# The long filter of a Hyena layer: hidden layers made inside the projection, sum and difference folded into the output weights, one sum over partitions

## The chip, the cores and the metric

The kernel runs on one core of one Trainium2 chip. The metric is the time of the whole kernel on the device, in microseconds. Three runs of the kernel before took 2927.18, 2945.96 and 2937.9 us, a median of 2937.9.

## The reference

The program is a two-layer encoder on 1024 positions of 1024 channels in float32: normalisation, a mixer, a residual, and a mixture of experts, twice. The mixer of the first layer is half attention and half a Hyena operator. The operator convolves a sequence `z` with a filter as long as the sequence, through Fourier transforms. The change concerns how this filter is computed:

```python
z = concat([t, cos(ang), -sin(ang)])          # (1024, 33), constants
hdn = sin(freq * (z @ w1 + b1))               # (1024, 64)
hdn = sin(freq * (hdn @ w2 + b2))             # (1024, 64)
filt = hdn @ w3                               # (1024, 2 * 512): forward and backward
decay = exp(-t * deltas)                      # (1024, 512)
h_fwd, h_bwd = filt[:, :512] * decay, filt[:, 512:] * decay
kern = concat([h_fwd.at[0].add(h_bwd[0]), zeros, h_bwd[:0:-1]])
kern = kern / (sum(abs(kern), axis=0) + EPS)
y = irfft(rfft(z_seq) * rfft(kern)) + z_seq * skip
```

For real transforms of both directions the kernel needs `hs = h_fwd + h_bwd` and `hd = h_fwd - h_bwd`, and for the division the sum of |h_fwd| + |h_bwd| over positions, in which position 0 counts as |h_fwd + h_bwd|.

## The kernel before

The kernel is a row of phases. Each phase is a function that writes one instruction list for each engine, with waits on semaphores by hand; it ends with `end_phase()`, a barrier of all engines. So work of two phases never overlaps, except that the big weights arrive through a ring of three chunks of 2 MB, refilled by SyncE as products finish (`refill`, L166).

Four phases matter here. `hyena_project` (L919) makes 12 blocks of the projection, three groups of four. A step is 48 matmuls of 512 columns into two of the PSUM banks 0 to 5; beside it ScalarE copies the block before into `up` and splits the next weights, VectorE runs the three-tap convolution (L1078 to L1091), and in the first eight steps the attention's output is normalised and transposed through banks 6 and 7 (`turn`, `move`). TensorE's list is: product i, then `turn(i)`.

`hyena_filter` (L1098) loads eight small tables on SyncE's queue (L1124), and all engines wait for all of them. TensorE then makes layer one, transposes half of `z` (`turn`), makes layer two, transposes the rest; VectorE brings each layer's argument into the range of the sine in six operations on 64 partitions of 1024 columns (L1242 to L1251), ScalarE takes the sine (L1212). Then come eight steps of 128 positions each: two filter matmuls with 64 rows (L1172), forward and backward; VectorE multiplies each by the decay (L1259, L1260) and forms sum and difference (L1261, L1262); ScalarE takes the sizes of both directions (L1198); TensorE sums them over partitions with a column of ones (L1162, `norm_sum`), two matmuls a step into one row. At the end this row becomes a column of reciprocals (L1264 to L1266), and ScalarE multiplies `z` by `skip` (L1226).

A float32 matmul shows as two records in the trace, each with its own weight load; those on `fp32r` data as one, and a transpose as one.

`hyena_forward` (L1276) loads transform tables piece by piece on SyncE's queue and makes 33 results, each evacuated by ScalarE (`keep`, L1338), from which VectorE forms four groups of products. `hyena_inverse` reads `z` for the skip term.

Of the kernel before, what the change touches and what calls it, by code (L numbers as in the profile page):

```python
# [8 lines left out]
F32R = mybir.dt.float32r  # L9
# [60 lines left out]
def build(nc, I, out):  # L70
    ctx = ExitStack()
    with ctx:
# [846 lines left out]
        def hyena_project(z, yT, xnH, o, gain, post):  # L919

            (proj, padded, convolved, weights_in, edges, chain, x_high, x_rest, w_high, w_rest,
             gain_in, squared, mean_ok, root_ok, scaled, turned, copied) = take(17)
            with ExitStack() as st:
# [7 lines left out]
                wH = sb(st, "w_high_hy", [P, 2, KD, P], F32R)  # L931
                STEPS = 3 * HC
                TURN = 6

# [13 lines left out]
                with nc.Block() as block:  # L948
                    @block.sync
                    def _(sp):  # L950
                        sp.dma_start(g_bc[:], gain.partition_broadcast(P)).then_inc(gain_in, 16)
                        sp.dma_start(cw[:], I["hy_conv_w"]).then_inc(weights_in, 16)
                        sp.dma_start(cb[:], I["hy_conv_b"]).then_inc(weights_in, 16)
                        refill(sp, S_HY, S_OUT0, proj, HC)

                    @block.tensor
                    def _(pe):
                        def turn(j):
# [6 lines left out]
                            last.then_inc(turned, 1)  # L965

                        for i in range(STEPS):
# [12 lines left out]
                            if i < NT:  # L980
                                turn(i)

                    @block.scalar
                    def _(act):
                        def squares(j):
# [32 lines left out]
                        for i in range(STEPS):  # L1018
# [11 lines left out]
                            if i < NT:  # L1030
                                move(i)

                    @block.vector
                    def _(dve):
                        did = Tally(chain)

# [33 lines left out]
                        for i in range(STEPS):  # L1070
# [27 lines left out]
        def hyena_filter(z, zT, hs, hd, hinv):  # L1098
            (tab_in, lin, argued, waved, filt, decayed, mixed, normed, turned, moved, skipped, chain,
             row_ok, summed, patched) = take(15)  # L1100
            with ExitStack() as st:
                zp = sb(st, "hy_positions", [EMB, T])
                w1 = sb(st, "hy_w1", [EMB, FF])
                w2 = sb(st, "hy_w2", [FF, FF])
                w3 = sb(st, "hy_w3", [FF, 2 * 512])
                fb = sb(st, "hy_fb", [FF, 3])
                tneg = sb(st, "hy_tneg", [P, NT])
                delta = sb(st, "hy_delta", [P, 512])
                skip = sb(st, "hy_skip", [P, HC])
                arg = sb(st, "hy_arg", [FF, T])  # L1110
                turns = sb(st, "hy_turns", [FF, T])
                hdn = sb(st, "hy_hidden", [FF, T])
                dec = sb(st, "hy_decay", [P, 2, 512])
                hf = sb(st, "hy_fwd", [P, 2, 512])
                hb = sb(st, "hy_bwd", [P, 2, 512])
                ab = sb(st, "hy_abs", [P, 2, 2, 512])
                row = sb(st, "hy_row", [1, 512])
                TWO_PI = 2 * np.pi
                HI = 6.28125
                LO = TWO_PI - HI  # L1120
                MAGIC = 1.5 * 2.0 ** 23
                with nc.Block() as block:
                    @block.sync
                    def _(sp):  # L1124
                        for t, src in ((zp[:], I["c_positions"]), (w1[:], I["hy_w1"]), (w2[:], I["hy_w2"]),
                                       (w3[:], I["hy_w3"]), (fb[:], I["hy_fb"]), (tneg[:], I["c_tneg"]),
                                       (delta[:], I["c_delta"].partition_broadcast(P)), (skip[:], I["hy_skip"])):
                            sp.dma_start(t, src).then_inc(tab_in, 16)

                    @block.tensor  # L1130
                    def _(pe):
                        def layer(w, x):
                            for half in range(2):
                                last = nc.tensor.matmul(psum[0:FF, half, :], w[:], x[:, half * 512:(half + 1) * 512],
                                                        start=True, stop=True)
                            last.then_inc(lin, 1)

                        def turn(n):
                            par, mt = divmod(n, NF)
                            if n >= 4:  # L1140
                                pe.wait_ge(moved, n - 3)
                            for ct in range(HC):
                                t0 = par + 2 * mt * P
                                last = nc.tensor.transpose(psum[:, 4 + n % 4, ct * P:(ct + 1) * P],
                                                           z[:, ct, t0:t0 + 2 * P - 1:2], ident[:])
                            last.then_inc(turned, 1)

                        pe.wait_ge(tab_in, 16 * 8)
                        layer(w1, zp)
                        for n in range(4):  # L1150
                            turn(n)
                        pe.wait_ge(waved, 1)
                        layer(w2, hdn)
                        for n in range(4, NT):
                            turn(n)
                        pe.wait_ge(waved, 2)
                        pe.wait_ge(moved, NT)

                        def norm_sum(n):
                            pe.wait_ge(mixed, n + 2)  # L1160
                            for d in range(2):
                                last = nc.tensor.matmul(psum[0:1, 4, :], ones[:, 0:1], ab[:, n % 2, d, :],  # L1162
                                                        start=(n == 0 and d == 0), stop=(n == NT - 1 and d == 1))
                            last.then_inc(normed, 1)

                        for n in range(NT):
                            par, mt = divmod(n, NF)
                            t0 = par + 2 * mt * P
                            if n >= 2:
                                pe.wait_ge(summed, n - 1)  # L1170
                            for half in range(2):
                                last = nc.tensor.matmul(psum[:, 2 * (n % 2) + half, :], hdn[:, t0:t0 + 2 * P - 1:2],  # L1172
                                                        w3[:, half * 512:(half + 1) * 512], start=True, stop=True)
                            last.then_inc(filt, 1)
                            if n:
                                norm_sum(n - 1)
                        norm_sum(NT - 1)
                        pe.wait_ge(row_ok, 1)
                        for ct in range(HC):
                            last = nc.tensor.matmul(psum[:, 5, ct:ct + 1], row[0:1, ct * P:(ct + 1) * P],  # L1180
                                                    ones[0:1, 0:1], start=True, stop=True)
                        last.then_inc(normed, 1)

                    @block.gpsimd
                    def _(pool_e):
                        pool_e.wait_ge(patched, 2)
                        nc.gpsimd.memset(ab[0:1, 0, 1, :], 0.0).then_inc(mixed, 1)

                    @block.scalar
                    def _(act):  # L1190
                        def size(n):

                            b = n % 2
                            act.wait_ge(summed, n + 1)
                            if n >= 2:
                                act.wait_ge(normed, n - 1)
                            for d, h in ((0, hf), (1, hb)):
# [1703 lines left out]
```

## Time and profile before

| | |
|---|---|
| median of three runs | 2937.9 us |
| the profiled execution | 2935.33 us, span 2933.5 us |
| TensorE matmul busy | 2554.4 us (87%) |
| VectorE busy | 1860.2 us (63%) |
| ScalarE busy | 1448.1 us (49%) |
| GpSimd busy | 441.0 us (15%) |
| mean granted TensorE clock | 0.927 |

Engines are named PE (TensorE), DVE (VectorE), ACT (ScalarE), POOL (GpSimd) and SP (SyncE); SPq is SyncE's queue of loads. Busy is the time in which instructions ran. A granted clock of 1.0 is 2.4 GHz, 0.5 is 1.2 GHz. In a timeline a row gives start and duration in us, engine, line, operation, output and inputs, the shape, how many instructions were merged (x), and in brackets how long the engine was idle before and what ended that. In a row of stretches the columns are: stretch, length, busy us and count of PE, PEld (weight loads), DVE, ACT and POOL, then granted clock, share of the DMA engines and GB/s.

### The profile page before, as it was taken

The numbers are of one execution on the slowest core, as the hardware profiler recorded it, in microseconds if no ns is written. First come the engines' busy times: TensorE is split into PE (matmuls) and PEld (weight loads), VectorE is DVE, ScalarE is ACT, GpSimd is POOL, SyncE is SP. The second block draws the span as 40 slices with busy tenths as digits, with TensorE's granted clock in tenths as the row PEclk, the third lists the DMA queues.
The fourth block names the chain that finished last, engine by engine and source line by source line (L and its number), as shares of the span: only waits on it lengthen the run. The fifth ranks groups of instructions, "written<-read, shape, count | busy, mean of one in ns | idle before, by whom it ended". The sixth has DMA issues, their size and how long they took to land. (4 is left out here: it accounts for less than half of the span.)

```text
span 2933.5 us, 34401 instructions
## 1 busy us (share of the span) xinstructions
PE 2554.4 (87%) x12440; PEld 2021.0 (69%) x12440; DVE 1860.2 (63%) x2221; ACT 1448.1 (49%) x1731; POOL 441.0 (15%) x396
## 2 busy tenths in 40 slices
PE   5989898797893999999985999879494899999994
PEld 4768786243571788888874899867382688888882
DVE  5748754455334888888874310079734789888980
ACT  4338731311220778878864222143511678877870
POOL 0001000000000133333310000012200233332320
PEclk9989998798996999999997999979697899999997
DMA  4110001011131899999992101200322699999992
GB/s 159 46 43 2 5 29 67 7 36 72 65 143 38 334 382 389 384 377 387 385 331 77 58 30 51 94 1 1 129 94 83 253 378 377 379 375 378 401 341 96
DMA packets 86674, 533.41 MB, mean 182 GB/s; under 512 B 18503, under 2 KB 24135, under 8 KB 61096
## 3 DMA queue, kind: packets, MB, share of 16 engines
q1 hardware_dynamic: 63240, 494.17, 42.8%
q0 software_dynamic: 18720, 33.61, 4.8%
q10 hardware_dynamic: 4608, 4.20, 0.4%
q8 instruction: 68, 1.11, 0.2%
q14 instruction: 38, 0.31, 0.0%
HBM read 511.45 MB, written 55.05 MB: 193 GB/s over the span
## 5 line engine op out<-in xcount | busy, mean ns | idle before, releaser
L1936 DVE TENSOR_TENSOR wL<-ring,wH 128x2048 fp32r<-128x2048 f32 x384 | 869.0, 2287 | 140.2 <-ACT wH L1883 134.8
L1883 ACT CAST wH<-ring 128x2048 fp32r<-128x2048 f32 x384 | 730.2, 1910 | 227.8 <-DMA ring<-in_moe_w 161.1
L1802 PE MATMUL psum<-wH,xgH 128*128 128x512 f32 x1024 | 408.4, 399 | 8.9 <-DVE xgL L1936 8.7
L1804 PE MATMUL psum<-wH,xgL 128*128 128x512 f32 x1024 | 401.4, 392 | 0.0
L1810 PE MATMUL psum<-wL,xgH 128*128 128x512 f32 x1024 | 274.7, 390 | 0.0
L1802 PEld LDWEIGHTS psum<-wH,xgH 128*128 128x128 f32 x1024 | 193.4, 189 | 52.3 <-DVE xgL L1936 7.8
L1810 PEld LDWEIGHTS psum<-wL,xgH 128*128 128x128 f32 x1024 | 192.5, 188 | 41.4
L1804 PEld LDWEIGHTS psum<-wH,xgL 128*128 128x128 f32 x1024 | 193.6, 189 | 38.5
L1802 PE MATMUL psum<-wH,hidH 128*128 128x512 f32 x512 | 207.7, 406 | 10.4 <-DVE hidL L1936 10.4
L1804 PE MATMUL psum<-wH,hidL 128*128 128x512 f32 x512 | 201.6, 394 | 0.0
L190 PE MATMUL psum<-w_high_vo,xn_high 128*128 128x256 f32 x512 | 144.1, 281 | 5.4 <-DVE ring_rest L185 5.4
L192 PE MATMUL psum<-w_high_vo,xnT_rest 128*128 128x256 f32 x512 | 144.3, 282 | 0.0
L191 PE MATMUL psum<-ring_rest,xn_high 128*128 128x256 f32 x512 | 144.2, 282 | 0.0
L1810 PE MATMUL psum<-wL,hidH 128*128 128x512 f32 x512 | 137.4, 390 | 0.0
L192 PE MATMUL psum<-xn_high,ring_rest 128*128 128x512 f32 x320 | 127.3, 398 | 0.0
L1757 POOL COPY gidx<-slots 128x1 int32 (+1 forms) x64 | 55.1, 860 | 479.7 <-PE psum L1819 479.5
L1802 PEld LDWEIGHTS psum<-wH,hidH 128*128 128x128 f32 x512 | 97.3, 190 | 29.8 <-DVE hidL L1936 10.9
L190 PE MATMUL psum<-w_high,xnT_rest 128*128 128x512 f32 x256 | 103.0, 402 | 14.4 <-DVE ring_rest L185 14.4
L1810 PEld LDWEIGHTS psum<-wL,hidH 128*128 128x128 f32 x512 | 96.8, 189 | 20.4
L1804 PEld LDWEIGHTS psum<-wH,hidL 128*128 128x128 f32 x512 | 97.6, 191 | 18.4
L191 PE MATMUL psum<-ring_rest,xnT_rest 128*128 128x512 f32 x256 | 101.7, 397 | 0.0
L192 PE MATMUL psum<-w_high,yT_rest 128*128 128x512 f32 x256 | 101.5, 397 | 0.0
(407 smaller groups left out, 4965.0 us busy)
## 6 DMA issues: line engine op xcount, KB each, us to landing
ring<-in_moe_w SPq DMA_DIRECT2D x192, 2048.0 KB
ring<-in_ev_w_in SPq DMA_DIRECT2D x6, 2048.0 KB
ring<-in_od_w_in SPq DMA_DIRECT2D x6, 2048.0 KB
xn_scratch<-xn_out SPq DMA_DIRECT2D x16, 512.0 KB, 3.6
ow<-in_moe_w SPq DMA_DIRECT2D x3, 2048.0 KB, 12.4
x_all<-in_x SPq DMA_DIRECT2D x4, 1024.0 KB, 8.1
ring<-in_ev_w_out SPq DMA_DIRECT2D x2, 2048.0 KB
dft_tables<-in_c_dft SPq DMA_DIRECT2D x16, 256.0 KB, 3.0
```

Of the source, the lines that this page charges most:

```text
L190: nc.tensor.matmul(dst, lhs[0], rhs[0], start=start, stop=False)
L191: nc.tensor.matmul(dst, lhs[0], rhs[1], start=False, stop=False)
L192: return nc.tensor.matmul(dst, lhs[1], rhs[0], start=False, stop=stop)
L1757: nc.gpsimd.tensor_copy(idx[:, b:b + 1], slots[:, bass.ds(e, 1)]).then_inc(idx_ok, 1)
L1802: nc.tensor.matmul(psum[:, bank, :], xh[:, k, :], w3[0][:, n, cols], start=(half == 0 and n == 0), stop=False)
L1804: nc.tensor.matmul(psum[:, bank, :], xl[:, k, :], w3[0][:, n, cols], start=False, stop=False)
L1810: ins = nc.tensor.matmul(psum[:, bank, :], xh[:, k, :], w3[1][:, n, cols], start=False, stop=(half == 1 and n == len(ks) - 1))
L1883: nc.scalar.copy(half_of(wH, b, e, c, half), raw(e, c, half)).then_inc(w_high, 1)
L1936: return nc.vector.tensor_tensor(out, whole, high.bitcast(F32), ALU.subtract)
```

## The change

It does five things. The two sine layers move into `hyena_project`: after the products of steps 7 to 10 TensorE makes one half (512 positions) of a layer each, with the weights doubled to 128 columns, so that the hidden values stand twice, on partitions 0 to 63 and 64 to 127; banks 6 and 7 and the buffer `sq` are reused. The tables are loaded there. The output weights are combined once: rows 0 to 63 of `w3` become forward plus backward, rows 64 to 127 forward minus backward. So in `hyena_filter` one matmul on the lower rows gives the sum and one on the upper rows the difference, and one product with the decay each gives `hs` and `hd`. The sizes are computed from |h_fwd| + |h_bwd| = max(|hs|, |hd|) (`both_abs`, `larger`), added up over the eight steps by GpSimd, and summed over partitions once. The transposes of `z` alternate with the filter matmuls, evacuated by ScalarE and VectorE in turn. The scaling by `skip` moves to pieces 3 to 6 of `hyena_forward`, with its load.

The diff, cut:

```diff
@@ hyena_project
+                        for t, src in ((zp, I["c_positions"]), (w1, I["hy_w1"]), (w2, I["hy_w2"]), (fb, I["hy_fb"]),
+                                       (w3, I["hy_w3"][0]), (tneg, I["c_tneg"]),
+                                       (delta, I["c_delta"].partition_broadcast(P))):
+                            sp.dma_start(t[:], src).then_inc(mlp_in, 16)
                         refill(sp, S_HY, S_OUT0, proj, HC)
...
+                        def hidden_layer(u):
+                            if u == 0:
+                                pe.wait_ge(mlp_in, 16 * 7)
+                            if u < 2:
+                                pe.wait_ge(copied, NT - 1 + u)
+                            else:
+                                pe.wait_ge(argued, u - 1)
+                                pe.wait_ge(waved, u - 1)
+                            w, x = (w1, zp) if u < 2 else (w2, hidden[0:FF, :])
+                            nc.tensor.matmul(psum[:, TURN + u % 2, :], w[:], x[:, piece(u)], start=True, stop=True
+                                             ).then_inc(lin, 1)
...
                             last.then_inc(proj, 1)
                             if i < NT:
                                 turn(i)
+                            if MLP <= i < MLP + 4:
+                                hidden_layer(i - MLP)
...
+                        def wave(u):
+                            act.wait_ge(argued, u + 1)
+                            nc.scalar.activation(hidden[:, piece(u)], sq[:, 0, :], ACT.Sin).then_inc(waved, 1)
...
+                            if i == MLP - 2:
+                                act.wait_ge(squared, NT)
+                                act.dma_start(w3b, I["hy_w3"][1]).then_inc(back_in, 16)
+                            if MLP <= i < MLP + 4:
+                                wave(i - MLP)
...
+                        def argument(u):
+                            V, k = nc.vector, u // 2
+                            arg, turns = sq[:, 0, :], sq[:, 1, :]
+                            dve.wait_ge(lin, u + 1)
+                            if u:
+                                dve.wait_ge(waved, u)
...
+                        def both_directions():
...
+                            for s, op in ((0, ALU.add), (1, ALU.subtract)):
+                                rows = slice(s * FF, (s + 1) * FF)
+                                nc.vector.tensor_tensor(w3[rows, :], w3[rows, :], w3b[rows, :], op).then_inc(summed, 1)
...
+                            if i == MLP - 1:
+                                both_directions()
+                                dve.wait_ge(squared, NT)
+                            if MLP <= i < MLP + 4:
+                                argument(i - MLP)
@@ hyena_filter, TensorE
+                        def filters(n):
...
+                            if n >= 2:
+                                pe.wait_ge(mixed, 2 * n - 2)
+                            for s in range(2):
+                                rows = slice(s * FF, (s + 1) * FF)
+                                last = nc.tensor.matmul(psum[:, 2 * (n % 2) + s, :], hidden[rows, t0:t0 + 2 * P - 1:2],
+                                                        w3[rows, :], start=True, stop=True)
                             last.then_inc(filt, 1)
...
+                        for n in range(NT):
+                            filters(n)
+                            turn(n)
+                        pe.wait_ge(gathered_up, NT - 1)
+                        nc.tensor.matmul(psum[0:1, SUM, :], ones[:, 0:1], total[:], start=True, stop=True
+                                         ).then_inc(normed, 1)
@@ hyena_filter, ScalarE
+                        decay(0)
+                        for n in range(NT):
+                            if n + 1 < NT:
+                                decay(n + 1)
+                            act.wait_ge(mixed, 2 * n + 2)
+                            if n >= 2:
+                                act.wait_ge(sized, n - 1)
+                            for s, h in ((0, hs), (1, hd)):
+                                nc.scalar.activation(both_abs[:, n % 2, s, :], h[:, n, :], ACT.Abs).then_inc(absolute, 1)
...
+                            if n % 2 == 0:
+                                act.wait_ge(turned, n + 1)
+                                nc.scalar.copy(zT[:, n, :], psum[:, 4, :]).then_inc(moved[0], 1)
@@ hyena_filter, GpSimd
+                        for n in range(1, NT):
+                            pool_e.wait_ge(sized, n + 1)
+                            if n > 1:
+                                pool_e.wait_ge(gathered_up, n - 1)
+                            nc.gpsimd.tensor_tensor(total[:], total[:], size[:, n % 2, :], ALU.add).then_inc(gathered_up, 1)
@@ hyena_filter, VectorE
+                        def larger(n):
+
+                            dve.wait_ge(absolute, 2 * n + 2)
+                            if n >= 3:
+                                dve.wait_ge(gathered_up, n - 2)
+                            nc.vector.tensor_tensor(size[:, n % 2, :] if n else total[:], both_abs[:, n % 2, 0, :],
+                                                    both_abs[:, n % 2, 1, :], ALU.max).then_inc(sized, 1)
+
                         for n in range(NT):
...
+                            nc.vector.tensor_tensor(hs[:, n, :], psum[:, 2 * b, :], dec[:, b, :], ALU.mult
+                                                    ).then_inc(mixed, 1)
+                            nc.vector.tensor_tensor(hd[:, n, :], psum[:, 2 * b + 1, :], dec[:, b, :], ALU.mult
+                                                    ).then_inc(mixed, 1)
+                            if n:
+                                larger(n - 1)
+                            if n % 2:
+                                dve.wait_ge(turned, n + 1)
+                                nc.vector.tensor_copy(zT[:, n, :], psum[:, 5, :]).then_inc(moved[1], 1)
@@ hyena_forward
+                        sp.dma_start(skip[:], I["hy_skip"]).then_inc(skip_in, 16)
                         for n in range(PIECES):
...
+                            if 3 <= n < 3 + HC:
+                                nc.scalar.activation(z[:, n - 3, :], z[:, n - 3, :], ACT.Copy, scale=skip[:, n - 3:n - 2]
+                                                     ).then_inc(skipped, 1)
```

## Rows read from the trace of the kernel before

**Rows 1.** Windows, projection and filter phase: stretch, length, busy us by engine.

```profile
367.50:493.80 126.30, 126.28 (x561) 101.94 (x558) 62.58 (x89) 32.92 (x84) 0.00 (x0) 1.00 0.09 34
499.10:576.60 77.50, 53.54 (x112) 18.33 (x112) 33.88 (x46) 27.48 (x41) 0.51 (x1) 0.70 0.05 16
```

**Rows 2.** Timeline of the filter phase: start us, us, engine, line, operation, [idle before].

```profile
497.03 1.28 DVE L1087 SCALAR_TENSOR_TENSOR yT<-u_padded,hy_conv_w,conv_acc 128x1024 f32<-128x1024 f32 x1
499.12 0.38 SPq L1128 DMA_DIRECT2D hy_positions<-in_c_positions  x1
...
505.85 3.67 PE L1134 MATMUL psum<-hy_positions,hy_w 33*64 33x512 f32 x4 [12.07 <-DMA hy_skip<-in_hy_skip]
...
521.72 3.69 PE L1144 MATMUL psum<-ident,z 128*128 128x128 f32 x16
...
530.97 7.16 PE L1172 MATMUL psum<-hy_w,hy_hidden 64*128 64x512 f32 x8 [5.56 <-ACT zT L1215]
```

**Rows 3.** Groups of instructions in the filter phase: busy, mean ns, idle before.

```profile
L1144 PE MATMUL psum<-ident,z 128*128 128x128 f32 x32 | 7.4, 422 | 0.0
...
L1219 ACT ACTIVATE hy_decay<-hy_delta,hy_tneg 128x512 f32<-128x512 f32 x8 | 5.6, 708 | 0.0
L1261 DVE TENSOR_TENSOR xnT<-hy_fwd,hy_bwd 128x512 f32<-128x512 f32 x8 | 5.5, 692 | 0.3
...
L1259 DVE TENSOR_TENSOR hy_fwd<-psum,hy_decay 128x512 f32<-128x512 f32 x8 | 5.5, 691 | 20.7 <-PE psum L1172 20.7
...
L1198 ACT ACTIVATE hy_abs<-hy_bwd 128x512 f32<-128x512 f32 x8 | 4.9, 612 | 0.0
...
L1219 ACT ACT_TABLE_LOAD x1 | 1.3, 1283 | 0.0
```

**Rows 4.** Timeline of the filter steps, TensorE.

```profile
550.07 1.99 PE L1172 MATMUL psum<-hy_w,hy_hidden 64*128 64x512 f32 x4
...
565.68 1.99 PE L1172 MATMUL psum<-hy_w,hy_hidden 64*128 64x512 f32 x4
```

**Rows 5.** Timeline, end of the filter phase.

```profile
571.54 4.25 ACT L1226 ACTIVATE z<-z,hy_skip 128x1024 f32<-128x1024 f32 x4
...
571.68 1.88 PE L1162 MATMUL psum<-hy_abs,ones 128*1 128x512 f32 x4 [2.21 <-ACT hy_abs L1198]
...
575.42 0.18 DVE L1266 RECIPROCAL hinv<-psum 128x4 f32<-128x4 f32 x1 [1.14 <-PE psum L1180]
```

**Rows 6.** Timeline, head norm of layer two, VectorE, then GpSimd.

```profile
2076.63 1.67 DVE L731 SCALAR_TENSOR_TENSOR xnT<-xnT,rs_ml,g_ml 128x256 f32<-128x256 f32 x4
...
2078.49 3.71 DVE L731 SCALAR_TENSOR_TENSOR xnT<-xnT,rs_ml,g_ml 128x256 f32<-128x256 f32 x4
...
2078.38 2.35 POOL L742 TENSOR_TENSOR xnT<-xnT,gate_ml 128x1024 f32<-128x1024 f32 x1 [28.84 <-DVE xnT L731]
```

**Rows 7.** Windows, TensorE alone: busy (records), PEclk the granted clock, DMA share.

```profile
498.00:500.00 2.00, 0.00 (x0) 0.53 1.07 459
524.50:525.50 1.00, 0.90 (x5) 0.54 0.00 0
531.00:538.20 7.20, 7.13 (x8) 0.50 0.00 0
550.00:571.00 21.00, 18.91 (x41) 1.00 0.00 0
```

**Rows 8.** Timeline of attention, TensorE.

```profile
254.36 0.40 PE L511 MATMUL psum<-k_high,q_rest 64*128 64x512 f32 x2
254.59 0.40 PE L511 MATMUL psum<-k_rest,q_high 64*128 64x512 f32 x2
```

**Rows 9.** Timeline of the forward transform, ScalarE and then VectorE.

```profile
641.27 0.66 ACT L1338 COPY filter_freq<-psum 128x512 f32<-128x512 f32 x1
...
696.11 2.50 DVE L1370 TENSOR_TENSOR freq_acc<-Z,filter_freq 128x512 f32<-128x512 f32 x4 [9.78 <-ACT filter_freq L1338]
```

More of the change, by code:

```diff
@@ L918, in hyena_project @@
         @phase
-        def hyena_project(z, yT, xnH, o, gain, post):
+        def hyena_project(z, yT, xnH, o, gain, post, hidden, consts):
             (proj, padded, convolved, weights_in, edges, chain, x_high, x_rest, w_high, w_rest,
-             gain_in, squared, mean_ok, root_ok, scaled, turned, copied) = take(17)
+             gain_in, squared, mean_ok, root_ok, scaled, turned, copied, mlp_in, lin, argued, waved, summed, back_in) = take(23)
+            w3, delta, tneg = consts
             with ExitStack() as st:
@@ L1093, in _, with hyena_filter @@
                                 scale(i + 1)
+                            if i == MLP - 1:
[3 more added lines that the diff above has]
+                                argument(i - MLP)
                 end_phase()
         @phase
-        def hyena_filter(z, zT, hs, hd, hinv):
-            (tab_in, lin, argued, waved, filt, decayed, mixed, normed, turned, moved, skipped, chain,
-             row_ok, summed, patched) = take(15)
-            with ExitStack() as st:
[L1102 to L1112, printed above, removed]
+        def hyena_filter(z, zT, hidden, consts, hs, hd, hinv):
+            (filt, decayed, mixed, absolute, sized, patched, gathered_up, normed, turned, moved0, moved1,
+             row_ok) = take(12)
+            moved = (moved0, moved1)
+            w3, delta, tneg = consts
+            with ExitStack() as st:
@@ L1120, in hyena_filter @@
-                LO = TWO_PI - HI
-                MAGIC = 1.5 * 2.0 ** 23
+                SUM = 6
                 with nc.Block() as block:
[L1123 to L1128, printed above, removed]
@@ L1130, in _ @@
                     @block.tensor
                     def _(pe):
[L1132 to L1164, printed above, removed]
@@ L1169, in _ @@
                             if n >= 2:
[L1170 to L1173, printed above, removed]
-                            last.then_inc(filt, 1)
-                            if n:
-                                norm_sum(n - 1)
@@ L1177, in _, with turn @@
-                        norm_sum(NT - 1)
+                                pe.wait_ge(mixed, 2 * n - 2)
[3 more added lines that the diff above has]
+                                                        w3[rows, :], start=True, stop=True)
+                            last.then_inc(filt, 1)
+                        def turn(n):
+                            par, mt = divmod(n, NF)
+                            if n >= 2:
+                                pe.wait_ge(moved[n % 2], n // 2)
+                            for ct in range(HC):
+                                t0 = par + 2 * mt * P
+                                last = nc.tensor.transpose(psum[:, 4 + n % 2, ct * P:(ct + 1) * P],
+                                                           z[:, ct, t0:t0 + 2 * P - 1:2], ident[:])
+                            last.then_inc(turned, 1)
@@ L1178, in _ @@
+                        for n in range(NT):
[4 more added lines that the diff above has]
+                                         ).then_inc(normed, 1)
                         pe.wait_ge(row_ok, 1)
                         for ct in range(HC):
-                            last = nc.tensor.matmul(psum[:, 5, ct:ct + 1], row[0:1, ct * P:(ct + 1) * P],
+                            last = nc.tensor.matmul(psum[:, SUM + 1, ct:ct + 1], row[0:1, ct * P:(ct + 1) * P],
@@ L1275, in hyena_forward @@
         @phase
-        def hyena_forward(zT, hs, hd, Z):
-            (done, copied, mixed, chain, early) = take(5)
+        def hyena_forward(z, zT, hs, hd, Z):
+            (done, copied, mixed, chain, early, skip_in, skipped) = take(7)
             BUFS = 2
```

141 lines of the change are left out of this document (58 added, 83 removed).

## The prediction

> **What bounds the kernel now.** I began with the busy time per stage, to find what the changed phases lean on. In the projection (`hyena_project`) TensorE is busy 126.28 of 126.30 us at full clock, so whatever is put on it there is paid in full; one of its eleven steps takes 126.3 / 11 = 11.5 us. In the filter phase (`hyena_filter`) it is busy 53.5 of 77.5 us at a mean clock of 0.70, and VectorE 33.9 us: nobody is full, the phase is a chain of hand-overs [rows 1]. All phases are closed by a barrier of all engines, and DMA moves next to nothing in the filter phase (share 0.05), so its length lies wholly on the kernel's time and no prefetch uses it.
>
> The timeline of the phase then gives its parts [rows 2]. The last convolution ends at 497.03 + 1.28 = 498.31, SyncE issues its first table at 499.12, the first matmul waits for the last of eight tables until 505.85 (6.7 us). The two sine layers run from there to 530.97, where the first filter matmul starts (25.1 us). Eight filter steps, the sums and the scaling by `skip` end at 571.54 + 4.25 = 575.79 [rows 2, 5]: 44.8 us. Together 76.7 us. A step in steady state repeats every (565.68 - 550.07) / 4 = 3.9 us [rows 4], although no engine has that much work in it: VectorE makes hf, hb, sum, difference, ScalarE takes the sizes, TensorE sums them, and each waits for the one before.
>
> **What goes, and what the new phase costs.** Tables and both layers leave the phase: 6.7 + 25.1 = 31.8 us. For the rest I build the new phase anew, since its bound changes. Per step TensorE has two filter matmuls (each two records in the trace, four together) and four transposes; VectorE two products of 0.69 and 0.68, one maximum (0.69, as the sum it resembles) and in every second step a copy out of PSUM, at most the 0.69 of a product: 2.4 us, say 2.5 with hand-overs; ScalarE a decay (0.71), two sizes (0.61 each) and half a copy of at most 0.66 [rows 9]: 2.3 us; GpSimd one addition of half of 2.35 = 1.2 us [rows 3, 6]. The sums over partitions, four records a step, shrink to one pair at the end.
>
> TensorE's clock decides what its part costs. After the projection's end the granted clock fell from 1.0 to 0.5 (1.2 GHz) within 5 us (mean 0.53 between 498 and 500), and the new phase starts about then, so I start it at 1.2 GHz. Eight records of the filter's 64-row matmuls without a break left it there, it was 1.00 later, with the 128-row sums between them [rows 7]. A record costs 7.16 / 8 = 0.90 us at 1.2 GHz [rows 2] and 1.99 / 4 = 0.50 at 2.4 GHz [rows 4]; a transpose 7.4 / 32 = 0.23 [rows 3], four of them 0.9.
>
> The change puts the second filter matmul on rows 64 to 127 of the array, the first on rows 0 to 63. In attention such pairs overlap: two records, one on each half (x2), follow the two before them after 0.23 us [rows 8], and a full-height record of as many columns takes as long in the projection, 126.3 / 561 = 0.23 [rows 1]. Here each matmul has two records on the same half, so I let the last of the first overlap with the first of the second: three slots in place of four. The bounds are two and four slots; I take three because the order of issue allows just that (two would end the phase 7 us earlier, four is case C).
>
> A step is then 3 x 0.90 + 0.9 = 3.6 us of TensorE, more than VectorE's 2.5 and ScalarE's 2.3: TensorE bounds it. From a start at 499.2 the last pair is done at 499.2 + 2.7 + 7 x 3.6 = 527.1. The loading of the exponential's table (1.28) and the first decay (0.7) [rows 3] lie beside the first 2.7 us; at the full clock, with 1.5 us of cover, they would show 0.5. Behind the last pair comes the tail: products 1.3, sizes 1.2, maximum 0.7, GpSimd's addition 1.2, one pair of sum records 1.8, and from there to the reciprocal what it takes now, 575.60 - (571.68 + 1.88) = 2.0 [rows 5]; with 0.2 for two more hand-overs 8.4. The phase ends at 535.5 in place of 575.8: **40.3 us less**.
>
> Additions elsewhere. **Projection:** four hidden matmuls of two records, 8 x 0.50 = 4.0 us on a full TensorE. Bounds: 3.8, at the 0.47 of a sum's record (1.88 / 4) [rows 5], and 6, if each matmul costs another half microsecond on changing from 128 to 33 or 64 rows, which no row excludes. What hangs on them: a layer takes 25.1 / 2 = 12.6 us now, 3.67 of it the matmuls; the rest, VectorE's six operations and the sine, is 8.9, so 4.5 for a half, and once a table load of 1.3. VectorE is busy 62.6 and ScalarE 32.9 of 126.3 us there [rows 1], 5.7 and 3.0 a step, so 4.5 more in an 11.5 us step is covered. A matmul of layer two stands two steps (23 us) behind the one whose sine it reads; that chain is at most 8.7 (all that both engines do in a step) + 4.5 + 1.3 = 15, so nobody waits. Were that cover gone, each of four stalls would cost up to 15. The combination of w3 (two operations) and seven loads on SyncE ahead of its refills (which wait for the fourth product, 46 us in) are covered too; so is the one load on ScalarE's queue, ordered one step before it is needed. **Forward transform:** the load of `skip` now stands ahead of the first table on SyncE, for which TensorE waits: 0.4 (as 499.12's row [rows 2]). The four scalings of z (4.25 in all) move to pieces 3 to 6. Three of them fall into ScalarE's catching up that ends at 641.27 + 0.66 and hold VectorE's second group back by 3.2 us; VectorE is idle 9.78 us before its last group, waiting for TensorE [rows 9], so this is hidden; without that it would cost 3.2. The clock at the start of the transform is low either way; how long it stays so may differ by up to 1.5 us, for which I take nothing.
>
> Sum: 40.3 - 4.0 - 0.4 = 35.9 us less. The profiled execution took 2935.3, 2.6 below the median of 2937.9; the new one would take 2899.4, and the median 2902.
>
> **A rule that speaks for the low clock.** In this trace the clock rose to 1.0 at about 525.4 (mean 0.54 from 524.5 to 525.5) when TensorE had done nothing but transposes for 3.7 us [rows 2, 7]. The Trainium skill ("TensorE: Matmul & The Clock Gate", Part 4) says that transposes do not engage the full clock, not counting as busy in the same way. By the rule the new phase would keep 1.2 GHz to its end, which is my forecast; by the row its transposes count and the clock may rise, which is the second case below.
>
> **The cases.**
> A (0.38), as above: 2902.
> B (0.26), the clock is at 2.4 GHz for most of the phase. The transposes on all 128 rows speak for it, and that the gap before the phase is 5 us and not the 12 of now; against it, that the 64-row records alone did not raise it. Then a step is bound by VectorE's 2.5: 499.2 + 2.0 + 7 x 2.5 = 518.7, tail 7.5, end 526.2, 49.6 less, net 45; with a rise only half way 40. 2893 to 2898.
> C (0.18), the two halves don't overlap: step 4.5, end 499.2 + 3.6 + 31.5 + 8.4 = 542.7, 33.1 less, net 28.7: 2909.
> D (0.05), GpSimd holds VectorE up. While POOL ran 2.35 us, VectorE's next operation with two SBUF inputs took until it was done or nearly: four together took 3.71 against 1.67 with POOL idle [rows 6]. Of the new phase's operations only the maximum has two SBUF inputs, and by order it comes 1.3 us (the two products) after POOL's start; POOL needs 1.2, so it is free. If the products were held too, a step would be 2.5 + 1.2 = 3.7: 2903. The Trainium skill ("GPSIMD Engine Reference", Key points) has VectorE and GpSimd share SBUF interfaces, with contention for two SBUF inputs; the row agrees.
> E (0.09), a cost that I don't see (changes between 64 and 128 rows, slower 64-row records, longer waits in the projection) eats 8 to 20 us: 2910 to 2922.
> F (0.04), slower. The hidden matmul stands in TensorE's queue ahead of the next product; if it has to wait for the sine chain of its own step and not of two before, TensorE stalls for 15 us four times, 60 in all: 2937.9 - 35.9 + 60 = 2962. It decides once the chain is longer than 23 us; my 15 speaks against it.
>
> From A, B, C and D come 2893 to 2909. With the spread of the runs of before (2927 to 2946, about 9 to a side of the median) and half of E, the range is 2887 to 2916. A measurement tells about 1% from nothing, 29.4 us: A, B and D are beyond it, C stands at it and is halved, E within, F slower. Faster 0.78, same 0.18, slower 0.04.
>
> **What would show it.** The filter phase should last 36 us from its first record to the reciprocal, with no table wait; filter records of the two halves should start in threes of slots at a granted clock of 0.5; the projection's steps 7 to 10 should be 1.0 longer each and TensorE idle in none of them; POOL's seven additions 1.2 each with no long maximum beside them; ScalarE's scalings in the forward transform with TensorE's pace there unchanged. A clock of 1.0 in the phase means B, a step of 4.5 means C, an idle TensorE in the projection F.

## The result and the profile after

The changed kernel takes **2892.4 us** (median of four, 2889.74 to 2899.33), the kernel before 2935.7 (median of four): a ratio of 0.986, interval 0.984 to 0.988. The forecast was 2902. The profiled execution took 2889.74, with a span of 2887.9.

The length of each phase, in us, from its first instruction to that of the next:

| | up to the projection | projection | filter | forward | all behind | span |
|---|---|---|---|---|---|---|
| before | 349.0 | 150.1 | 77.5 | 138.0 | 2218.9 | 2933.5 |
| changed | 345.0 | 154.2 | 30.1 | 139.2 | 2219.3 | 2887.9 |

The filter phase gave 47.4 us back, the projection took 4.1 and the forward transform 1.2: 42.1 net. The spans differ by 45.6: 4.0 more are saved in code that nobody touched, ahead of the projection, and about 0.4 is lost behind the transform. The part ahead of the projection lay between 344.5 and 350.1 us in the twelve profiles of this study, so it is no effect of the change.

The windows of the changed kernel, with the columns of [rows 1]: the projection, the start of the filter phase, its steps, its tail, and the start of the forward transform.

```profile
367.00:494.00 127.00, 126.90 (x550) 99.89 (x548) 75.74 (x113) 33.35 (x79) 0.00 (x0) 1.00 0.10 36
499.26:504.00 4.74, 4.70 (x12) 1.77 (x12) 1.29 (x2) 3.77 (x5) 0.00 (x0) 0.50 0.24 100
504.00:518.00 14.00, 11.70 (x54) 5.77 (x52) 12.40 (x21) 11.06 (x20) 5.11 (x4) 1.00 0.00 0
518.00:529.30 11.30, 3.73 (x10) 1.86 (x10) 5.28 (x9) 2.77 (x5) 3.79 (x3) 0.64 0.00 0
532.90:538.20 5.30, 5.27 (x7) 2.20 (x8) 0.00 (x0) 0.00 (x0) 0.00 (x0) 0.51 0.01 4
```

TensorE is as full in the projection as it was, so the hidden matmuls stall nothing. At the start of the filter phase the low clock lasts 4.7 us and no more (it is back in the tail, where TensorE waits: 0.64 as a mean). In the steps VectorE, not TensorE, is then the fullest engine (12.40 of 14.00 us). The timeline shows the same; first the start on TensorE:

```profile
499.30 2.08 PE L1192 MATMUL psum<-hy_w,hy_hidden 64*128 64x512 f32 x4 [5.40 <-PEq L102]
501.31 1.12 PE L1202 MATMUL psum<-ident,z 128*128 128x128 f32 x4
502.36 1.93 PE L1192 MATMUL psum<-hy_w,hy_hidden 64*128 64x512 f32 x4
...
504.89 1.14 PE L1192 MATMUL psum<-hy_w,hy_hidden 64*128 64x512 f32 x4
```

Four filter records take 2.08 us at 1.2 GHz and 1.14 at 2.4, where [rows 4] has 1.99 for four at 2.4: the halves overlap almost wholly. Now two steps of VectorE, and GpSimd beside them:

```profile
512.02 1.28 POOL L1250 TENSOR_TENSOR hy_size_sum<-hy_size_sum,hy_size 128x512 f32<-128x512 f32 x1 [0.63 <-DVE hy_size L1259]
512.47 0.67 DVE L1266 TENSOR_TENSOR xnT<-psum,hy_decay 128x512 f32<-128x512 f32 x1
...
513.07 0.67 DVE L1268 TENSOR_TENSOR xnT<-psum,hy_decay 128x512 f32<-128x512 f32 x1
513.66 0.67 DVE L1259 TENSOR_TENSOR hy_size<-hy_abs 128x512 f32<-128x512 f32 x1
...
514.26 0.68 DVE L1266 TENSOR_TENSOR xnT<-psum,hy_decay 128x512 f32<-128x512 f32 x1
...
514.87 0.67 DVE L1268 TENSOR_TENSOR xnT<-psum,hy_decay 128x512 f32<-128x512 f32 x1
...
515.46 0.78 DVE L1259 TENSOR_TENSOR hy_size<-hy_abs 128x512 f32<-128x512 f32 x1
...
516.16 0.68 DVE L1274 COPY zT<-psum 128x512 f32<-128x512 f32 x1
...
516.77 0.67 DVE L1266 TENSOR_TENSOR xnT<-psum,hy_decay 128x512 f32<-128x512 f32 x1
```

No VectorE row has an idle time in brackets: VectorE runs without a break, two steps in 516.77 - 512.47 = 4.3 us. Over the phase a step takes (518.56 - 501.42) / 7 = 2.45, since the first ones wait for other engines. The tail, all engines:

```profile
518.56 0.68 DVE L1266 TENSOR_TENSOR xnT<-psum,hy_decay 128x512 f32<-128x512 f32 x1
...
519.76 0.77 DVE L1259 TENSOR_TENSOR hy_size<-hy_abs 128x512 f32<-128x512 f32 x1
519.87 1.15 ACT L1234 ACTIVATE hy_abs<-xnT 128x512 f32<-128x512 f32 x2 [0.18 <-DVE xnT L1268]
520.45 0.68 DVE L1274 COPY zT<-psum 128x512 f32<-128x512 f32 x1
520.61 1.26 POOL L1250 TENSOR_TENSOR hy_size_sum<-hy_size_sum,hy_size 128x512 f32<-128x512 f32 x1 [0.63 <-DVE hy_size L1259]
521.05 1.37 DVE L1259 TENSOR_TENSOR hy_size<-hy_abs 128x512 f32<-128x512 f32 x1
522.50 1.26 POOL L1250 TENSOR_TENSOR hy_size_sum<-hy_size_sum,hy_size 128x512 f32<-128x512 f32 x1 [0.63 <-DVE hy_size L1259]
523.81 1.87 PE L1210 MATMUL psum<-hy_size_sum,ones 128*1 128x512 f32 x2 [5.88 <-POOL hy_size_sum L1250]
...
526.45 1.86 PE L1214 MATMUL psum<-ones,hy_row 1*128 1x1 f32 x8 [0.77 <-DVE hy_row L1277]
528.35 0.18 DVE L1279 RECIPROCAL hinv<-psum 128x4 f32<-128x4 f32 x1 [1.95 <-PE psum L1214]
```

### The profile page after: what moved, and what is told of

It is laid out like the page before. It is cut to its first block and busy times, and to the rows that moved or that the text cites. A ratio compares the mean times of both kernels' runs of the same rounds, so it can differ in the third digit from the quotient of the medians.

```text
span 2887.9 us, 34372 instructions
## 1 busy us (share of the span) xinstructions
PE 2521.1 (87%) x12410; PEld 2012.1 (70%) x12410; DVE 1862.0 (64%) x2231; ACT 1446.6 (50%) x1729; POOL 463.1 (16%) x402
## 5 line engine op out<-in xcount | busy, mean ns | idle before, releaser
L1955 DVE TENSOR_TENSOR wL<-ring,wH 128x2048 fp32r<-128x2048 f32 x384 | 869.4, 2288 | 139.3 <-ACT wH L1902 134.2
L1776 POOL COPY gidx<-slots 128x1 int32 (+1 forms) x64 | 63.9, 999 | 481.2 <-PE psum L1838 481.0
L1790 POOL COPY yidx<-slots 128x1 int32 (+1 forms) x64 | 92.0, 1437 | 66.2 <-DMA out<-y,yidx 36.9
L185 DVE TENSOR_TENSOR ring_rest<-ring,w_high_vo 128x2048 fp32r<-128x2048 f32 x8 | 18.3, 2292 | 129.4 <-ACT w_high_vo L2410 129.4
```

Of the source, the lines that this page charges most:

```text
L185: return nc.vector.tensor_tensor(out, whole, high.bitcast(F32), ALU.subtract)
L1776: nc.gpsimd.tensor_copy(idx[:, b:b + 1], slots[:, bass.ds(e, 1)]).then_inc(idx_ok, 1)
L1790: nc.gpsimd.tensor_copy(yidx[:, b:b + 1], slots[:, bass.ds(e, 1)]).then_inc(yidx_ok, 1)
L1955: return nc.vector.tensor_tensor(out, whole, high.bitcast(F32), ALU.subtract)
```

## The experiments

Whole times are ratios to the kernel before on the same chip; the phase lengths of each kernel are from its profile, measured as in the table above. The first two take the change apart.

**The layers alone**, steps of the filter phase as before (`skip` is loaded in the projection too, the scaling by it stays in the filter phase):

```diff
 hyena_filter, SyncE
+                        sp.dma_start(w3back[:], I["hy_w3"][1]).then_inc(tab_in, 16)
 hyena_filter, TensorE (no tables, no layers; all transposes ahead)
+                        for n in range(NT):
                             turn(n)
+                        pe.wait_ge(tab_in, 16)
```

The first form left the backward weights' load out; both matmuls of a step read the forward weights:

> Only the first part of the change: both sine layers in the projection, the eight filter steps, the sums over partitions and the scaling by skip as before (both matmuls of a step read the forward weights on rows 0 to 63, so the backward filter is left out). The eight groups of transposes stand ahead of the steps. Theory 1 (the two parts add up, each is worth what its chain took): the filter phase shrinks from 77.5 us by 31.8 and grows by up to 7.4 of uncovered transposes, and the clock, risen in the transposes, saves up to 7 us in the first steps: a phase of 46 to 53 us; the projection is 4.1 longer; the whole 20 to 27 us less than before, ratio 0.991 to 0.993. Rival (the hand-overs of the steps hid part of the layers' chain): less than 15 us, ratio above 0.995.

Measured: 2959.0, ratio 1.011 (1.008 to 1.013). The projection and filter phases took 4.4 more and 29.4 less, as expected, but the whole is not shorter. The time came back at the end of the kernel, from the load of expert weights for the overflow of the routing on. That row, and then its counterpart in the changed kernel:

```profile
2862.83 46.95 SPq L2041 DMA_DIRECT2D ow<-in_moe_w  x6
```
```profile
2840.84 1.30 SPq L2043 DMA_DIRECT2D ow<-in_moe_w  x3
```

From it to the end of the span are 2957.6 - 2862.8 = 94.8 us, against 47.1. The load runs six times and not three, and TensorE has 120 matmul records in this stretch and not 60: twice the work for the overflow. I read it as other values routing other tokens to the experts; to part the values from the schedule, the same edit ran again with nothing left out:

> The first experiment again with nothing left out: the backward weights are loaded at the head of the filter phase, beside the transposes, so its whole time can be read too. The first experiment's stretches gave a phase of 48.1 us and a projection 4.4 us longer. Theory 1 (the layers' part is worth about 25 of the 42 us): the same phase, whole time 23 to 27 us less than before, ratio 0.991 to 0.992. Rival (the length of the first experiment outside these phases, 48 us more, belongs to the edit): the whole is slower than before.

Measured: 2915.2, ratio 0.994 (0.992 to 0.996), everything behind the filter phase as long as before (to 0.5 us in each part), with three loads again. The filter phase fell by 29.2 to 48.3, the projection rose by 4.6. So the 50 us of the run before came with its values, not its schedule, and the rival "slower" falls. The whole gained 18 where 23 to 27 were expected and the phases say 24; its interval reaches from 13 to 23, and whether there is a rest, and where it went, is open. The profiled executions differ by 22.8.

**The steps alone**, with tables and both layers at the head of the new filter phase:

```diff
 hyena_filter, TensorE
+                        pe.wait_ge(tab_in, 16 * 8)
+                        layer(w1, zp)
+                        pe.wait_ge(waved, 1)
+                        layer(w2, hidden[0:FF, :])
```

> Only the second part: the new filter steps (sum and difference by two 64-row matmuls on the two halves of the rows, sizes by a maximum, added by GpSimd, summed once), but the tables and both sine layers stay at the head of the filter phase, on 128 partitions. Theory 1: the phase is the changed kernel's 30.1 us and some 31 of tables and layers, 61 us, 16 less than before's 77.5; ratio 0.994 to 0.995; with the first experiment's gain it adds up to the 42 us of the change. Rival (the steps gain only because the clock is up when they start): the phase is longer than 65 us and the two gains add up to less than 35.

Measured: 2915.0, ratio 0.995 (0.994 to 0.997). Filter phase 59.9, that is 17.6 less. In the filter phase the parts add up: 29.2 + 17.6 = 46.8 of the 47.4 us. The whole times don't show it: 18 + 14 = 32 us of 43, with intervals of 13 to 23, 8 to 19 and 36 to 46.

**No overlap**: both matmuls of a step on rows 0 to 63.

```diff
-                                last = nc.tensor.matmul(psum[:, 2 * (n % 2) + s, :], hidden[rows, t0:t0 + 2 * P - 1:2],
-                                                        w3[rows, :], start=True, stop=True)
+                                last = nc.tensor.matmul(psum[:, 2 * (n % 2) + s, :], hidden[0:FF, t0:t0 + 2 * P - 1:2],
+                                                        w3[0:FF, :], start=True, stop=True)
```

> The changed kernel with both filter matmuls of a step on rows 0 to 63 (the difference is left out, both make the sum), so that they can't overlap. Theory 1 (the halves overlap wholly, and with all rows at work the clock rises): four slots in place of two; the granted clock stays at 0.5 in the filter phase, a step takes about 4.4 us and the phase 42 to 45 us, 12 to 15 more than the changed kernel's 30.1. Theory 2 (the transposes alone raise the clock, the halves do not matter for it): the clock rises to 1.0 about as before, the step is 2.6 us and the phase 32 to 35.

Measured: 2908.2, ratio 0.992 (0.990 to 0.994), filter phase 47.9. Its TensorE rows, and the window over all of its steps:

```profile
504.09 3.75 PE L1192 MATMUL psum<-hy_w,hy_hidden 64*128 64x512 f32 x4 [5.40 <-PEq L102]
507.77 1.13 PE L1202 MATMUL psum<-ident,z 128*128 128x128 f32 x4
508.83 3.78 PE L1192 MATMUL psum<-hy_w,hy_hidden 64*128 64x512 f32 x4
```
```profile
504.00:544.00 40.00, 38.17 (x64) 15.12 (x64) 17.15 (x28) 17.93 (x30) 7.12 (x6) 0.50 0.03 15
```

One edit, two effects: four records take 3.75 us in place of 2.08, and the clock stays at 1.2 GHz although TensorE is busy 95% of 40 us. A step is 508.83 - 504.09 = 4.74 us where 4.4 were expected, and the phase is longer than the 42 to 45 expected. Without the overlap it is 17.8 us longer, clock included, and so hardly shorter than with the old steps (48.3 in the run before last, where the transposes stand ahead): what the new steps gain hangs on the halves. The shares of overlap and clock don't add. By my estimate the overlap alone, with the 3.06 us of the first step at 1.2 GHz (499.30 to 502.36 in the changed kernel), would save 7 x 1.7 = 12 us; the clock alone, which would halve the 4.74 to 2.37 against VectorE's 2.15, would save all but some 1.5 us. That the use of both halves raised the clock is shown; whether it is the overlap in time or the work on the upper rows isn't.

**Transposes first**, then all filter matmuls (the copies out of PSUM move ahead with them):

```diff
                         for n in range(NT):
+                            turn(n)
+                        for n in range(NT):
                             filters(n)
-                            turn(n)
```

> The changed kernel with all eight groups of transposes ahead of the eight pairs of filter matmuls, evacuated first. Theory 1 (transposes count for the clock as other work on all rows): the clock rises to 1.0 within some 4 to 7 us of the phase's start, while only transposes have run; the pairs then follow at VectorE's pace of about 1.8 us and the phase takes 31 to 33 us, 1 to 3 more than the changed kernel's. Rival, the page's rule (transposes don't engage the full clock): the clock stays at 0.5 for the whole 8 us of transposes and rises only in the pairs.

Measured: 2897.0, ratio 0.988 (0.986 to 0.991), filter phase 33.8, somewhat above the 31 to 33 expected. TensorE's first rows, and the windows over them:

```profile
504.25 6.14 PE L1202 MATMUL psum<-ident,z 128*128 128x128 f32 x28 [5.40 <-PEq L102]
510.58 0.75 PE L1202 MATMUL psum<-ident,z 128*128 128x128 f32 x4 [0.19 <-DVE zT L1265]
```
```profile
504.00:509.00 5.00, 4.75 (x21) 3.88 (x22) 1.38 (x2) 1.17 (x2) 0.00 (x0) 0.50 0.27 115
509.00:510.00 1.00, 1.00 (x7) 0.95 (x8) 0.17 (x1) 0.58 (x1) 0.00 (x0) 0.79 0.00 0
510.00:511.00 1.00, 0.81 (x7) 0.62 (x6) 0.52 (x1) 0.57 (x1) 0.00 (x0) 1.00 0.00 0
```

The clock rose with nothing but float32 transposes behind it.

**A busy gap**: 40 transposes of the identity on TensorE between projection and filter phase, while VectorE ends the convolution.

```diff
+                        pe.wait_ge(argued, 4)
+                        for k in range(40):
+                            last = nc.tensor.transpose(psum[:, TURN, 0:P], ident[:], ident[:])
```

> The changed kernel with 40 transposes of a constant into a free bank behind the last product of the projection, so that TensorE works through the 5.4 us gap ahead of the filter phase. Theory 1 (the low clock at the phase's start costs what its rows show: 2.0 and 1.9 for the first two pairs against 1.14): the granted clock is 1.0 from the phase's first record, the first products come 0.7 us and the second 1.5 us earlier, and the phase is 1.0 to 1.7 shorter than 30.1, since VectorE and the decays follow. Rival (the first decays set the start): nothing gained, 29.8 to 30.3.

Measured: 2890.7, ratio 0.985 (0.983 to 0.987), filter phase 28.4, 1.7 less (without the gap's work it was 30.1 and 30.2 in two profiles; the whole times can't tell so little apart). The first filter records already take 1.14 us:

```profile
503.37 1.14 PE L1196 MATMUL psum<-hy_w,hy_hidden 64*128 64x512 f32 x4 [1.03 <-PEq L102]
```

**The sum on VectorE**: GpSimd's additions become a seventh kind of operation in VectorE's list.

```diff
-                            nc.gpsimd.tensor_tensor(total[:], total[:], size[:, n % 2, :], ALU.add).then_inc(gathered_up, 1)
...
+                                nc.vector.tensor_tensor(total[:], total[:], size[:, n % 2, :], ALU.add).then_inc(gathered_up, 1)
```

> The changed kernel with the seven additions of the sizes on VectorE in place of GpSimd, behind each maximum. Theory 1 (a step is bound by VectorE's list, 0.6 us per operation, and not by TensorE): six of the seven additions lengthen the steps by 0.7 each, the last is 0.6 cheaper than GpSimd's and the last maximum is not held up (0.7): the phase is 3 us longer than 30.1. Rival (GpSimd holds VectorE up so much that its help is worth nothing): the phase is as long as before or shorter, 28 to 30 us.

Measured: 2900.3, ratio 0.988 (0.986 to 0.990), filter phase 33.6, 3.5 more. The first and the last product of the steps, then the tail:

```profile
505.62 0.69 DVE L1261 TENSOR_TENSOR xnT<-psum,hy_decay 128x512 f32<-128x512 f32 x1 [2.98 <-PE psum L1192]
...
526.72 0.68 DVE L1261 TENSOR_TENSOR xnT<-psum,hy_decay 128x512 f32<-128x512 f32 x1
...
529.94 0.68 DVE L1248 TENSOR_TENSOR hy_size<-hy_abs 128x512 f32<-128x512 f32 x1
530.75 0.69 DVE L1255 TENSOR_TENSOR hy_size_sum<-hy_size_sum,hy_size 128x512 f32<-128x512 f32 x1
531.50 1.87 PE L1210 MATMUL psum<-hy_size_sum,ones 128*1 128x512 f32 x2 [6.52 <-DVE hy_size_sum L1255]
```

The steps take 526.72 - 505.62 = 21.1 us in place of 17.1, 4.0 more for the additions between them. The tail is 0.5 shorter: the last maximum, with no GpSimd beside it, and the last addition, on VectorE, together take 1.2 less from start to start, and the maximum starts 0.7 later, since an addition and a copy stand ahead of it. VectorE's list does set the step.

**Tables early**: the first two tables of the forward transform and `skip` are loaded in the filter phase.

```diff
 hyena_filter, SyncE
+                        for n in range(2):
+                            sp.dma_start(tab[:, n, :, :], I["c_dft"][0, :, n, :, :]).then_inc(early_in, 16)
+                        sp.dma_start(skip[:], I["hy_skip"]).then_inc(early_in, 16)
```

> The changed kernel with the first two tables of the forward transform and the load of skip ordered at the head of the filter phase. Theory 1 (the transform's start waits for its own loads alone): TensorE starts 0.1 instead of 3.6 us after the phase's first instruction; the transform shrinks from 139.2 by 3.6 to 4.2 us, ratio to before 0.984 to 0.986. Rival (the same time goes into a longer stretch at the low clock): it shrinks by less than 2.

Measured: 2886.5, ratio 0.984 (0.982 to 0.987). The transform shortened by 3.5 to 135.7 us, a little under the expectation.

**All of it**: the busy gap and the early tables, the closing sum taken in two matmuls so that GpSimd's last addition falls away, transposes ahead of it, and the correction for position 0 one step later. Beside it ran the changed kernel once more.

```diff
+                        for k in range(24):
+                            nc.tensor.transpose(psum[:, SUM + 1, 0:P], ident[:], ident[:])
+                        pe.wait_ge(gathered_up, NT - 2)
+                        nc.tensor.matmul(psum[0:1, SUM, :], ones[:, 0:1], total[:], start=True, stop=False)
+                        pe.wait_ge(sized, NT)
+                        nc.tensor.matmul(psum[0:1, SUM, :], ones[:, 0:1], size[:, (NT - 1) % 2, :], start=False, stop=True
...
-                            if n == 0:
+                            if n == 1:
...
-                        for n in range(1, NT):
+                        for n in range(1, NT - 1):
```

> The changed kernel with the busy gap and the early tables together; besides, 24 transposes of a constant ahead of the closing sum, the last size summed by TensorE directly as a second matmul into the same row (GpSimd adds one less), and the correction of position 0 one step later on ScalarE. Theory 1 (the parts add up): the filter phase 28.4 less 1.3 (correction), 2.0 (GpSimd's last addition and the held maximum) and 1.8 (closing at the full clock instead of 0.5), 23 to 24.5 us; the transform 135.7 less up to 2 for the full clock at its start, 133.5 to 135.7; the whole 10 to 13 us below the changed kernel, ratio to before 0.980 to 0.983. Rival (the closing matmuls wait for the dummy transposes, or the clock falls all the same): the phase 26 us or more.

> The changed kernel once more beside the combined one: a phase of 30.1, a transform of 139.2, ratio 0.985 to 0.987; what differs from the first profile outside these is the spread of unchanged code.

Measured: 2877.3, ratio 0.981 (0.979 to 0.983), against 2895.1, ratio 0.987 (0.984 to 0.989), of the changed kernel measured beside it. Filter phase 24.6 (30.2 beside it), transform 134.8 (139.3): 10 us are in the phases, as expected (the filter phase just above the 23 to 24.5); the medians differ by 18. In the two profiled executions (16.3 apart) 5.0 of the rest lie ahead of the projection, in code that is the same in both; I take the rest as such spread, which isn't shown for the medians. The closing rows:

```profile
518.41 1.37 DVE L1274 TENSOR_TENSOR hy_size<-hy_abs 128x512 f32<-128x512 f32 x1
...
519.28 1.02 PE L1223 MATMUL psum<-hy_size_sum,ones 128*1 128x512 f32 x2 [1.39 <-POOL hy_size_sum L1265]
520.13 1.02 PE L1225 MATMUL psum<-hy_size,ones 128*1 128x512 f32 x2
...
521.92 1.05 PE L1229 MATMUL psum<-ones,hy_row 1*128 1x1 f32 x8 [0.77 <-DVE hy_row L1292]
```

The closing matmuls run at 2.4 GHz: a sum takes 1.02 us and the turn into a column 1.05, not 1.87 and 1.86. The last maximum still takes 1.37.

## Why the prediction was right, and where it was not

The number held, inside the range and 10 us from the median, but the mechanism on which it was built, case A, did not. This is case B, at 0.26 the second of the cases: the range took it in, and to that the forecast owes its being right. Case B had 45 us net for an early rise (2893) and 40 for a late one; the phases gave 42.1, between the two, and the median of 2892.4 has 3 us of other code in it.

**Tables and layers out**: right. Forecast 31.8 us, the experiment shows 29.2 of phase; that phase without layers also has the transposes in the open, which the layers had hidden.

**Three slots of four**: failed. The step argued that two records on the same half leave one slot unshared. Four records take 2.08 us at 1.2 GHz with the halves and 3.75 without: 2.2 slots, close to the lower of the two bounds. The order of issue, from which the three were reasoned, didn't hold the second pair back. Case C, no overlap, falls with the same rows.

**The clock stays low**: failed, and by the prediction's own prices this is the larger term (49.6 - 40.3 = 9.3 us from A to B, against 7 for two slots). It rose 4.7 us into the phase. The forecast drew on eight 64-row records on one half that had left the clock down [rows 7], and applied them to pairs on both halves with transposes between. What the runs show: half-height records one at a time, with single groups of transposes between them, never raised it in 40 us; overlapped pairs with transposes did after 4.7 us; transposes alone did after 5.2 (504.25 to 509.4). The Trainium skill ("TensorE: Matmul & The Clock Gate", Part 4) says that transposes do not engage the full clock. Here they do (0.50, 0.79, 1.00 in the windows of the run with transposes first), and the measurement decides. The rise at 525.4 in the kernel before, on which the prediction leaned, was weaker evidence than it says, since the matmuls of layer two stood right ahead of the transposes:

```profile
518.11 3.67 PE L1134 MATMUL psum<-hy_hidden,hy_w 64*64 64x512 f32 x4 [4.98 <-ACT hy_hidden L1212]
521.72 3.69 PE L1144 MATMUL psum<-ident,z 128*128 128x128 f32 x16
```

**VectorE's 2.5 as the bound of case B**: right as a number, 2.45 as a mean, but two errors meet in it. In the steady steps it is 2.15: an operation of 0.68 follows the one before it after 0.60. The rest is lost at the start, where the second step comes 2.9 after the first at the low clock, and in the next one decay 2 on ScalarE stands behind the correction for position 0, which waits for a maximum; that step took 508.08 - 504.34 = 3.7.

**The tail**: too short. Forecast 8.4 in A and 7.5 in B, from the last pair; measured from VectorE's last L1266, 528.53 - 518.56 = 10.0. Two things were missing. The last maximum took 1.37 in place of 0.68, as POOL was adding from 520.61 to 521.87; its place behind maximum 6 and a copy cost nothing, as the sizes were ready only at 521.02. And TensorE, which waits 5.88 us for the last addition, was back at the low clock: the closing sum took 1.87, as A had it and B not, and the turn into a column, at 2.4 GHz in the kernel before, cost 0.8 more, in A too. The last experiment has both at 2.4 GHz and some 0.8 cheaper each.

**Case D**: right as far as it goes. The products out of PSUM took 0.67 to 0.68 with POOL busy beside them; the maxima that overlap with an addition are held: by 0.1 to 0.2 where they meet its end (0.86, 0.78 and 0.77), by 0.7 at the last. The other three of the seven meet none and take 0.67 to 0.68. The row of the head norm [rows 6] has two SBUF inputs under a far longer addition.

**Projection**: right. 4.1 for the forecast 4.0, with TensorE never idle. In the ten profiles with the layers in it the projection took 154.2 to 154.7 us, in the two without 150.1 and 149.6, so 5 isn't excluded. F needed a stall there and E an unseen cost of 8 to 20 us; neither is in the trace.

**Forward transform**: nearly right. 1.2 us for the forecast 0.4. The scalings of z are not seen in it. TensorE starts 0.5 us later in the phase (3.6 for 3.1), behind the load of `skip`, and the low clock at its start lasts 5.2 us against 3.8 before, worth half of the difference, 0.7; the prediction had named up to 1.5 us and taken none.

The sum again, with what was measured: 47.4 - 4.1 - 1.2 = 42.1, for 40.3 - 4.0 - 0.4 = 35.9. The 6.2 us between them are the clock and the overlap (36.3 of phase forecast, 29.3 measured from first record to reciprocal, the longer tail in it), less the dearer transform; the other 3.4 us to the median are within the spread of the runs.

## What to carry to other kernels

Where matmuls use 64 rows, try independent ones on the two halves of the array: here the time of both was nearly that of one, and the clock came with it. The rearranged steps gained 17.6 us with the halves, and hardly anything without them (47.9 against 48.3). When a phase is shortened, sum the work of each engine again and then look at its tail: here TensorE, idle for 5.88 us, had lost its clock, and the last maximum ran into GpSimd's second last addition. The layers moved under a full TensorE cost little more than their own records (4.1 us for 4.0), with two steps between a matmul of layer two and the one whose sine it reads; a shorter distance wasn't tried.

## What the chip showed that was not expected

- Float32 transposes alone raised the granted clock from 0.50 to 1.00 after 5.2 us; matmuls on one half with a few transposes between them, TensorE 95% busy, did not in 40 us.
- Forty useless transposes in a gap of 5 us kept the clock at 1.00, and the phase behind it ran 1.7 us faster.
- In the last experiment the clock was 1.00 up to 524.0, and then fell at the start of the transform all the same (mean 0.72 from 524 to 530), after 1.08 us of idle and with TensorE 99% busy. Ahead of it stood the closing matmuls, which use one column or one row of the array (519.28 to 522.97). Whether they let the clock fall is open.
- A maximum with two SBUF inputs that started 0.44 us after a GpSimd addition took 1.37 us, against 0.68 without one; it ended 0.55 after the addition. Products with one PSUM input took 0.68 either way.
